# Samples' attention: value pages four at a time in four column groups, the own key's term on VectorE, pages summed in the column sums

## What is computed

```python
kg = jnp.where(in_past, ck[page, off], k[bi, nidx])
vg = jnp.where(in_past, cv[page, off], v[bi, nidx])
logits = jnp.einsum('bqhd,bqkhd->bqhk', q, kg) * (DH_A ** -0.5) + bias
p = jax.nn.softmax(logits, axis=-1)
att = jnp.einsum('bqhk,bqkhd->bqhd', p, vg)
```

## Time and profile before

| what | value |
|---|---|
| median of 3 runs | 3496.82 us |
| the three runs | 3498.91, 3495.24, 3496.82 us |
| span of the profiled execution, first to last instruction | 3498.3 us |
| the profiled execution's own time | not listed apart from the runs |
| TensorE busy, share of the span | 3327.0 us, 95% |
| VectorE, ScalarE, GpSimd busy | 1548.7, 1136.8, 1193.4 us |
| mean granted TensorE clock | 0.964 of 2.4 GHz |

### The profile page before, as it was taken

The page is one execution under the profiler, slowest core; times in us unless marked ns, Lnnn a source line. Parts: engine busy times, 40 slices in busy tenths (PEclk is TensorE's granted clock), DMA queues, the critical chain, the costliest instruction groups (busy, mean ns, idle before and its releaser), DMA issues. The chain is left out here.

```text
span 3498.3 us, 57209 instructions
## 1 busy us (share of the span) xinstructions
PE 3327.0 (95%) x20524; PEld 3111.2 (89%) x20524; DVE 1548.7 (44%) x2743; ACT 1136.8 (32%) x2093; POOL 1193.4 (34%) x882
## 2 busy tenths in 40 slices
PE   7889989888999999999999999999899999999998
PEld 7469964676999999999899889899889999999998
DVE  3799972532321212122456776676752212212122
ACT  3412212442331212222345454555532322222122
POOL 2217832211322221222435566655453222222122
PEclk9989989885999999999999999999999999999998
DMA  4127653221311111111222322122432111111111
GB/s 134 52 30 156 198 178 112 61 78 50 56 49 48 45 46 48 48 42 48 92 73 93 98 78 92 56 92 80 165 105 73 49 48 42 49 48 44 46 48 67
DMA packets 344005, 263.87 MB, mean 75 GB/s; under 512 B 52134, under 2 KB 308150, under 8 KB 341910
## 3 DMA queue, kind: packets, MB, share of 16 engines
q1 hardware_dynamic: 327926, 232.18, 22.5%
q0 software_dynamic: 8192, 19.13, 1.6%
q10 hardware_dynamic: 7776, 11.09, 1.4%
HBM read 219.43 MB, written 44.76 MB: 76 GB/s over the span
## 5 line engine op out<-in xcount | busy, mean ns | idle before, releaser
L234 POOL TENSOR_TENSOR w_low_sb<-w_loaded_sb,w_high_sb 128x1024 fp32r<-128x1024 f32 (+1 forms) x278 | 568.4, 2052 | 1550.5 <-ACT w_high_sb L226 1532.6
L252 PE MATMUL psum<-act_high_sb,w_high_sb 128*128 128x344 f32 (+1 forms) x2400 | 769.7, 321 | 10.2 <-PEq L985 6.0
L252 PE MATMUL psum<-act_low_sb,w_high_sb 128*128 128x344 f32 (+1 forms) x2400 | 768.1, 320 | 0.0
L252 PE MATMUL psum<-act_high_sb,w_low_sb 128*128 128x344 f32 (+1 forms) x2400 | 767.8, 320 | 0.0
L252 PE MATMUL psum<-second_high_sb,w_high_sb 128*128 128x344 f32 x1728 | 553.3, 320 | 0.5 <-PEq L2301 0.5
L252 PE MATMUL psum<-second_low_sb,w_high_sb 128*128 128x344 f32 x1728 | 551.9, 319 | 0.0
L252 PE MATMUL psum<-second_high_sb,w_low_sb 128*128 128x344 f32 x1728 | 551.9, 319 | 0.0
L252 PEld LDWEIGHTS psum<-act_high_sb,w_high_sb 128*128 128x128 f32 (+1 forms) x2400 | 450.8, 188 | 11.5 <-issue 10.2
L252 PEld LDWEIGHTS psum<-act_high_sb,w_low_sb 128*128 128x128 f32 (+1 forms) x2400 | 451.3, 188 | 0.4
L252 PEld LDWEIGHTS psum<-act_low_sb,w_high_sb 128*128 128x128 f32 (+1 forms) x2400 | 450.9, 188 | 0.4
L226 ACT CAST w_high_sb<-w_loaded_sb 128x1024 fp32r<-128x1024 f32 (+1 forms) x230 | 239.6, 1043 | 519.1 <-PE psum L252 497.8
(11 more groups left out here) (437 smaller groups left out, 4912.0 us busy)
## 6 DMA issues: line engine op xcount, KB each, us to landing
w_loaded_sb<-in_w_up SPq DMA_DIRECT2D x64, 512.0 KB, 4.1
w_loaded_sb<-in_w_down SPq DMA_DIRECT2D x64, 512.0 KB, 4.2
w_loaded_sb<-in_w_in_odd SPq DMA_DIRECT2D x48, 512.0 KB, 4.0
key_pages_sb<-in_cache_k SPq DMA_DIRECT2D x64, 256.0 KB, 2.8
ecay_sum_spread_sb<-decay_sum_scratch SPq DMA_DIRECT2D x8, 2048.0 KB, 9.6
w_loaded_sb<-in_w_in_even SPq DMA_DIRECT2D x28, 512.0 KB, 4.0
gated_scratch<-gated_sb POOLq DMA_DIRECT2D x8, 1032.0 KB, 4.4
ample_ssm_state_sb<-in_state_ssm SPq DMA_DIRECT2D x64, 128.0 KB, 7.0
```

The costliest lines, as they stand in the source:

```text
L234: ins = self.nc.gpsimd.tensor_tensor(self.wl[:, par, k, 0:width], self.wf[:, par, k, 0:width], self.wh[:, par, k, 0:width].bitcast(F32), A ...
L252: ins = nc.tensor.matmul(out, w[:, par, k, 0:width], a[:, k, cols], start=n == 0, stop=n == 3 * KT - 1)
```

## The change

Per half of four pages there are now four matmuls with the same stationary 128 x 32 (four pages times eight heads), each with one page as the moving operand and its output in another group of 32 partitions: 0 to 31, 32 to 63, 64 to 95, 96 to 127. Of the 32 rows in group t only the 8 that belong to page t are wanted. The two halves of a sample add up in the same bank. `pick` (128 x 8, made of four pieces of the identity) marks for partition 40 t + h that head h is wanted; VectorE multiplies with it while it keeps each head's columns, now on 128 partitions. The sum over partitions by `to_columns` then also sums the pages. Its result goes to the first four columns of the sample's own bank, and VectorE copies it to `att`. Banks are now 1, 5 and 3 by turns. Half m is multiplied at step m * 7 // 4 + 1, so the last at step 27 and not 29.

The own term leaves TensorE: VectorE multiplies the own values with the own probabilities at step 17 of `keys_and_values` (`ownv`, two operations) and makes `pick` there (four), and adds `ownv` once at step 32. `pownd` and its matmul go. The waits at `dot(32)` and `turn(32)` now ask for the seventh and the eighth sample's copy.

```diff
@@ probs_dve
         if n == 14:
             dve.wait_ge(self.s_exp, 2)
             dve.wait_ge(self.s_mxt, 1)
-            nc.vector.tensor_tensor(self.pownd[:], self.pown[0:NS, :].rearrange("p (b h) -> p b h", b=NS), eye8,
-                                    ALU.mult).then_inc(self.s_pownd, 1)
@@ probs_dve, n == 17, behind the reciprocal
+            for e in range(2):
+                r = slice(64 * e, 64 * e + 64)
+                step(nc.vector.tensor_tensor(self.ownv[r, :, :], B.qkv[r, 8:12, SEQ:TOK],
+                                             self.pown[r, :].rearrange("p (b t e) -> p e t b", b=NS, e=2)[:, e], ALU.mult))
+            step(nc.vector.tensor_copy(self.pick[:], B.ident[:, 0:HA]))
+            for t in range(1, 4):
+                step(nc.vector.tensor_tensor(self.pick[:], self.pick[:], B.ident[:, 40 * t:40 * t + HA], ALU.add))
@@ values_pe and its helpers (the old body of the loop over pages is gone)
+    def halves_at(self, n):
+        return [m for m in range(self.HALVES) if m * 7 // 4 + 1 == n]
+    def last_at(self, b):
+        return (2 * b + 1) * 7 // 4 + 1
+    def bank(self, b):
+        return self.BANKS[b % 3]
...
+        for m in self.halves_at(n):
+            b, u = m // 2, m % 2
+            pe.wait_ge(self.s_value[m % self.VRING], 16 * self.HALF * (m // self.VRING + 1))
+            if u == 0 and b >= 3:
+                pe.wait_ge(self.s_colk, b - 2)
+            w = self.logit[:, b, self.HALF * u:self.HALF * (u + 1), :].rearrange("p j h -> p (j h)")
+            for t in range(self.HALF):
+                ins = nc.tensor.matmul(B.psum[32 * t:32 * t + 32, self.bank(b), :], w, self.place(m)[:, t, :],
+                                       start=u == 0, stop=u == 1)
+            ins.then_inc(self.s_taken, 1)
         for b in range(NS):
-            if n == self.ready(b) + 2:
+            if n == self.last_at(b) + 2:
                 self.to_columns(pe, b)
@@ to_columns
-            ins = nc.tensor.matmul(B.psum[:, 5, b * 4 + t:b * 4 + t + 1], self.own_cols[:, b % 2, t * P:(t + 1) * P],
-                                   B.ones[0:HA, 0:1], start=True, stop=True)
+            ins = nc.tensor.matmul(B.psum[:, self.bank(b), t:t + 1], self.own_cols[:, b % 2, t * P:(t + 1) * P],
+                                   B.ones[:, 0:1], start=True, stop=True)
@@ values_dve
-            if n == self.ready(b) + 1:
-                dve.wait_ge(self.s_pvd, b + 1)
+            if n == self.last_at(b) + 2:
+                dve.wait_ge(self.s_taken, 2 * b + 2)
...
+                nc.vector.tensor_tensor(self.own_cols[:, b % 2, :].rearrange("p (g d) -> p g d", g=HA),
+                                        B.psum[:, self.bank(b), :].rearrange("p (g d) -> p g d", g=HA),
+                                        self.pick[:].unsqueeze(2).to_broadcast([P, HA, DH]), ALU.mult).then_inc(self.s_kept, 1)
+            if n == self.last_at(b) + 4:
+                dve.wait_ge(self.s_col, b + 1)
+                nc.vector.tensor_copy(self.att[:, :, b], B.psum[:, self.bank(b), 0:4]).then_inc(self.s_colk, 1)
+        if n == self.last_at(NS - 1) + 5:
+            dve.wait_ge(self.s_colk, NS)
+            done(dve, nc.vector.tensor_tensor(self.att[:], self.att[:], self.ownv[:], ALU.add), self.s_step)
@@ attend, dot and turn
-                    pe.wait_ge(smp.s_kept, NS)
+                    pe.wait_ge(smp.s_colk, NS - 1)
...
-                    pe.wait_ge(smp.s_att, 2)
+                    pe.wait_ge(smp.s_colk, NS)
```

More of the change, by code:

```diff
@@ L1287 @@
     FIRST = 7
-    STEPS = 30
+    BANKS = (1, 5, 3)
     def __init__(self, B):
@@ L1297, in __init__ @@
         (self.s_mt, self.s_owned, self.s_ob, self.s_own, self.s_logit, self.s_pmax, self.s_mxt, self.s_dmax, self.s_mb,
-         self.s_sub, self.s_exp, self.s_pownd, self.s_part, self.s_sum, self.s_den) = (B.sem(x) for x in (
+         self.s_sub, self.s_exp, self.s_part, self.s_sum, self.s_den) = (B.sem(x) for x in (
              "mask_turned", "own_logits", "own_spread", "own_logits_kept", "sample_logits", "page_max", "max_turned",
-             "max_diagonal", "max_spread", "max_subtracted", "sample_probs", "own_probs_diagonal", "page_sums",
+             "max_diagonal", "max_spread", "max_subtracted", "sample_probs", "page_sums",
              "probs_summed", "denominator"))
-        self.s_taken, self.s_pvd, self.s_kept, self.s_col, self.s_att, self.s_high = (B.sem(x) for x in (
-            "value_page_weighed", "sample_values", "own_columns_kept", "columns_summed", "sample_att", "sample_att_high"))
+        self.s_taken, self.s_kept, self.s_col, self.s_colk, self.s_att, self.s_high = (B.sem(x) for x in (
+            "value_pages_weighed", "own_columns_kept", "columns_summed", "columns_kept", "sample_att", "sample_att_high"))
         self.s_step = B.tally("sample_step")
@@ L1311, in __init__ @@
         self.pown = B.take("own_prob_sb", [P, NS * HA])
-        self.pownd = B.take("own_prob_diagonal_sb", [NS, NS, HA])
+        self.pick = B.take("own_head_of_tile_sb", [P, HA])
+        self.ownv = B.take("own_values_weighed_sb", [P, 4, NS])
         self.pmax = B.take("page_max_sb", [P, NS * HA])
@@ L1487, in load_values @@
         self.load_pages(eng, "cache_v", self.place(m), m, self.s_value[m % self.VRING])
+    def halves_at(self, n):
[4 more added lines that the diff above has]
+        return self.BANKS[b % 3]
     def values_pe(self, pe, n):
         B, nc = self.B, self.B.nc
[L1492 to L1504, removed]
+        for m in self.halves_at(n):
[8 more added lines that the diff above has]
+            ins.then_inc(self.s_taken, 1)
         for b in range(NS):
-            if n == self.ready(b) + 2:
+            if n == self.last_at(b) + 2:
                 self.to_columns(pe, b)
-    def ready(self, b):
-        p = b * PAGES + PAGES - 1
-        return next(n for n in range(self.STEPS) if (n + 1) * NS * PAGES // self.STEPS > p)
     def to_columns(self, pe, b):
@@ L1526, in values_dve @@
         for b in range(NS):
-            if n == self.ready(b) + 1:
-                dve.wait_ge(self.s_pvd, b + 1)
+            if n == self.last_at(b) + 2:
+                dve.wait_ge(self.s_taken, 2 * b + 2)
                 if b >= 2:
                     dve.wait_ge(self.s_col, b - 1)
[L1531 to L1535, removed]
+                nc.vector.tensor_tensor(self.own_cols[:, b % 2, :].rearrange("p (g d) -> p g d", g=HA),
[7 more added lines that the diff above has]
+            done(dve, nc.vector.tensor_tensor(self.att[:], self.att[:], self.ownv[:], ALU.add), self.s_step)
             for e in range(2):
                 r = slice(64 * e, 64 * e + 64)
[L1538 to L1542, removed]
+                nc.vector.tensor_tensor(self.att[r, :, :], self.att[r, :, :],
+                                        self.den[r, :].rearrange("p (b t e) -> p e t b", b=NS, e=2)[:, e],
+                                        ALU.mult).then_inc(self.s_att, 1)
+        if n == self.last_at(NS - 1) + 8:
             dve.wait_ge(self.s_high, 1)
@@ L1547, in values_act @@
     def values_act(self, act, n):
-        if n == self.STEPS + 3:
+        if n == self.last_at(NS - 1) + 6:
             act.wait_ge(self.s_att, 2)
@@ L1772, in attend @@
     o = B.take("att_rows_sb", [P, 512])
-    smp.own_cols = B.take("own_columns_sb", [HA, 2, 512])
+    smp.own_cols = B.take("own_columns_sb", [P, 2, 512])
     seq = [(i, h) for i in range(NBLK) for h in range(HA)]
```

## The result

The changed kernel took 3463.63 us (median of four runs, 3449.78 to 3465.25) against 3497.86 for the kernel before, four runs on the same chip: ratio 0.9895, 95% interval 0.9875 to 0.9915. By the ratio that is 37 us less, by the two medians 34; 36 were predicted, and a time of 3461. Run again beside the experiments (e8), it gave 3458.36 us and 0.9890 (0.9873 to 0.9908). The profiled execution took 3462.52 us, of which the span is 3460.9.

What follows compares the result with a forecast made beforehand. TensorE was taken to bound the attention block's first half. Of 50.1 us less work, chain and loads leave 34.6 gained to head 32 (1.3 paid), plus 1.4 after: 36.0, from 3496.8 to 3461 us; range 3452 to 3473.

Steps and rivals of the forecast that it cites:

- R1: Rival, chance 0.07: four column groups don't overlap at all, a burst costs 3.53 us, gain 6.6 us, time 3490.
- R2: Rival, chance 0.05: weight loads lie bare, each of eight even bursts 0.8 us longer, 6.4 us in all, time 3467.
- two at once: Variant within the forecast's range: only two page matmuls overlap, a burst lasts 1.81 us, 6.9 us more, time 3468.
- 50 us of TensorE work aren't the gain: Value pages and own terms: 50.1 us of TensorE work go, but something else is late next; gain to head 32 34.6.
- The chain's length: Attention block to head 32: logit pairs 59.2 us, even bursts 7.6, column sums 3.9, together 70.7 us at full clock.
- The loads as a floor: Attention block: the last four pages land at 581.8 us, so head 32's products can't start before 590.6.
- The 1.3 us ahead of the block: Step 17 before attention: six small VectorE operations added, one gone from step 14; uncovered, everything after moves by 1.3 us.
- The pair after head 32: Pair from 628.63 to 636.15, 7.5 us: freed of the last sample's columns and scaling wait, 6.1, so 1.4 more gained.
- Every later stretch as long as now: Sign: stretches after head 32 keep their length; prediction wrong if one after 640 us changes by over 5 us.
- R3: Rival, chance 0.10: clock falls more in the thinned stretch; low for half of it 3470, for all of it 3487.
- R4: Rival, chance 0.06: the clock, once down, stays down through the whole attention block; slower, time 3517.
- R5: Rival, chance 0.05: shifted arrival raises retention's clock, 780 to 860 us, from 0.57 to 0.85; about 28 us go, 3433.

Runs made afterwards that it cites:

- e8: The changed kernel itself, run again beside the experiments: 3458.36 us, ratio 0.9890 to the kernel before.
- e2: Changed kernel with all four page matmuls of a half in one group of output partitions: 3495.15 us, ratio 0.9985 to the kernel before.
- e3: Changed kernel with the four page matmuls of a half by turns in two groups of output partitions: 3470.97 us, ratio 0.9919 to the kernel before.
- e4: Changed kernel with only the first page of each half multiplied, page loads unchanged: 3457.23 us, ratio 0.9882 to the kernel before.
- e6: Changed kernel with half 5 loaded by ScalarE's queue at the end of `keys_and_values`, steps unchanged: 3456.78 us, ratio 0.9891 to the kernel before.
- e9: Changed kernel with bursts behind odd heads and halves 5 and 6 loaded by GpSimd's queue at the start of `keys_and_values`: 3456.14 us, ratio 0.9884.
- e12: Changed kernel with bursts behind odd heads, half 5 loaded by ScalarE's queue, half 6 late by GpSimd's, both in `keys_and_values`: 3457.97 us, ratio 0.9893.
- e5: Changed kernel with the bursts of halves 3 to 15 at odd steps, behind odd heads, loads unchanged: 3462.72 us, ratio 0.9896 to the kernel before.
- e7: Changed kernel with bursts behind odd heads and half 5 loaded early by ScalarE's queue: 3455.63 us, ratio 0.9884 to the kernel before.
- e11: Changed kernel with the own key's term back on TensorE, four groups kept: 3478.91 us, ratio 0.9945 to the kernel before.

## Why the prediction was right, and where it was off

- **Four groups at once: shown.** 1.00 us a burst where 0.95 was taken, linear in the number of groups (e2, e3), weight loads beside the matmuls (e4). R1 and R2 are out, and "two at once" is e3: 3471 against 3468 forecast.
- **50 us of TensorE work aren't the gain: shown.** In the stretch TensorE's busy time fell by 46.7 us (115.61 to 68.96), and 38.9 came out of it. The chain between engines ends last: taking away three more matmuls of four (e4) or bringing loads forward (e6) changes nothing, moving bursts and column sums to odd heads with the loads mostly out of the way takes 6.6 us (e9, e12). The prediction puts 11.5 us of them on the chain; e5's expectation leaves 8 of these behind odd heads.
- **The chain's length.** The prediction has head 32 at 594.0, 81.4 us after a first product at 512.55 (511.25 in the trace of before, and 1.3), at a clock of 0.85. Measured 78.5 at a clock of 0.93 (0.89 over 511 to 592, where the sign was "near 0.85"), 82.9 at 0.85 (e8). The prediction's own sum at these clocks is 584.9 - 512.55 + 0.14 x 0.5 x 70.7 = 77.3 and 72.35 + 10.6 = 83.0. So chain and clock together account for both to about 1 us, and the clock is the part that differs between executions. Two things in this are luck. First, these sums hold 1.65 us that do not belong there: the prediction begins the chain at SyncE's first issue (512.9) and not at the first product. Without them they are 75.7 and 81.3, 2.9 and 1.6 short; VectorE's new work within the block, which the prediction puts at nothing and at most 2 us, may be in that, and no run measures it apart. Second, 594.0 follows from none of the prediction's sums (595.5, 589.4, floor 590.6); the measured stretches lie on both sides of it. The price of the low clock itself: 4.4 us between the two executions, where TensorE's half doubled gives 5.7 and the measured pairs of the earlier trace rows give 2.4.
- **The loads as a floor: not confirmed.** 590.6 was the floor and "TensorE waits for page loads at steps 16 to 27" the sign. It waited once, 0.37 us, at step 23. The floor was sized well, 590.6 - 512.55 = 78.1 where 78.5 was measured, but it is not what set the time: with the loads 6 us earlier the stretch is the same (e6). The loads stay a near second: move bursts and column sums off the chain and TensorE waits for pages (4.9 us in e5, 3.0 in e7).
- **The 1.3 us ahead of the block: shown**, 1.30 in VectorE's timeline, 1.05 in the ledger.
- **The pair after head 32**: 595.14 to 600.84 is 5.7 us where 6.1 was said, against 7.5 of the earlier trace rows; the next is 6.1 against 7.4. By there 3.1 us are won and not 1.4; the second part as a whole gives back 2, where low spells fall otherwise (clock 0.87 before, 0.89 after).

Timeline of the changed kernel, the pairs behind head 32's:

```profile
600.84 1.36 PE L1840 MATMUL psum<-qkv_sb 64*128 64x512 f32 x8
606.91 1.36 PE L1840 MATMUL psum<-qkv_sb 64*128 64x512 f32 x8
```

- **"Every later stretch as long as now"**: held within 3 us in the first execution. In e8 the second part is 5.3 us shorter, just over the 5 us that the prediction had named as a sign of being wrong; the bound was tighter than the clock lets such a stretch repeat. R3's 3470 and 3487, R4 and R5 didn't come: the low share of the stretch was 14% and 30%, and the clock rose again by itself each time. e11 is the warning that R3's mechanism is real: same chain, a little more TensorE work, 0.76 and 20 us.
- **Not in the prediction**: 4.3 us lost near 300 us in unchanged code, a load that came late. The block alone gained about 40 us (117.38 + 139.78 against 217.2 and 217.4) where 37.3 was forecast; the profiled execution came out close partly because the loss stood against that, which is luck. Whether the other runs behind the median lost the same 4.3 us is not recorded.

## What to carry to other kernels

Small matmuls that use few output columns are worth sending to different groups of 32 output partitions: four cost what one does here (1.00 against 0.97 us), also with full rows and own weight loads. Before counting the saved time, find what is late next: here the chain between engines took over after 39 of 47 us, with a DMA queue's issue rate just behind, so that earlier loads alone gave nothing and bursts moved off the chain alone only met waits for pages. Price such a chain at both levels of the clock and expect the same stretch of one kernel to differ between executions by a low spell, here by 4.4 us.

## What the runs showed of the hardware that was not expected

- Four groups run at once nearly without loss and without bare weight loads: 3.55, 1.84 and 1.00 us for one, two and four groups, 0.97 for one matmul alone.
- The same instructions met different low spells: 82.88 and 78.51 us for one stretch of one kernel, and 131.8 to 139.7 us for the second part, which is the same code in all changed kernels (clock 0.95 to 0.88).
- A wait of 2.0 us was followed by some 7 us at 1.2 GHz (e7), one of 1.44 us by none (e9).
- Adding 8 us of TensorE work to a thinned stretch cost 12 to 18 us of time in each of five runs against the changed kernel's first median, 18 to 23 against e8's (e11). Why the clock stayed down is open.
- Loads put on a third queue were not free where stores ran: at 395 GB/s a ring of buffers was held up by 7.6 us (e9). Issued late on GpSimd's queue, they left the stores alone and GpSimd's DRAIN at the end of the block took 6.04 us (e12).
